# Which partitions an expert's 64 slots stand on: rank order against an order in which eight neighbours in rank lie four partitions apart

## The reference, cut to what matters

```python
gp = softmax(ht @ w_group + b_group);  p_top, g_idx = top_k(gp, 1)         # one group a token
el_sel = (ht @ w_expert + b_expert) of that group
top_l, e_idx = top_k(el_sel, 2)                                            # two experts in it
gates = one_hot(group) x (softmax(top_l) * p_top at e_idx)                 # 512 x 32
for each expert e:  z = silu(ht @ wg) * (ht @ wu);  y += gates[:, e] * (z @ wd)
```

## Time and profile before

| | |
|---|---|
| median of 3 runs | 1217.79 us |
| profiled execution | 1218.0 us, span 1216.3 us |
| TensorE matmul busy | 1144.7 us (94%) |
| VectorE / ScalarE / GpSimd busy | 528.5 / 425.1 / 205.8 us |
| memory read / written | 265.84 MB / 30.41 MB |
| mixture of layer 0 | from about 500 to 746 us of the span |
| mixture of layer 1 | from about 964 to 1208 us of the span |

### The profile page before, as it was taken

The page is one execution under the profiler, slowest core; times in us unless marked ns, Lnnn a source line. Parts: engine busy times, 40 slices in busy tenths (PEclk is TensorE's granted clock), DMA queues, the critical chain, the costliest instruction groups (busy, mean ns, idle before and its releaser), DMA issues.

```text
span 1216.3 us, 29422 instructions
## 1 busy us (share of the span) xinstructions
PE 1144.7 (94%) x12512; PEld 626.1 (51%) x12512; DVE 528.5 (43%) x988; ACT 425.1 (35%) x823; POOL 205.8 (17%) x234
## 2 busy tenths in 40 slices
PE   6999999999999989899998889999999999998885
PEld 5365555555555644555554445544554555554442
DVE  6756564664565510511111125899941511111125
ACT  5335354454453421322121124555443321211123
POOL 3000000000000000222221110688800112221110
PEclk9999999999999989999999999999999999999898
DMA  4017311011012168799999998226702889999996
GB/s 162 3 55 294 126 50 42 21 59 42 20 59 72 74 216 330 283 358 420 423 420 422 424 376 339 70 74 255 311 0 75 324 307 425 420 422 422 422 402 255
DMA packets 53779, 281.97 MB, mean 232 GB/s; under 512 B 14956, under 2 KB 17132, under 8 KB 36496
## 3 DMA queue, kind: packets, MB, share of 16 engines
q1 hardware_dynamic: 43952, 263.73, 54.2%
q0 software_dynamic: 9408, 16.32, 3.7%
q10 hardware_dynamic: 288, 0.03, 0.0%
HBM read 265.84 MB, written 30.41 MB: 244 GB/s over the span
## 4 chain that ended last, share of the span: by engine, by line
PE 79%; DMA 13%; DVE 3%; ACT 2%; issue 2%; SPq 1%; DVEq 0%
PE psum L1611 15%; PE psum L976 14%; PE psum L2145 9%; PE psum L2443 8%; PE psum L1792 6%; PE psum L989 6%; DMA h<-rows 5%; DMA big<-in_moe_w_gate_up_dram 4%; DMA h<-in_moe_w_gate_up_dram 4%; PE psum L943 2%; PE psum L1916 1%; PE psum L1781 1%; PE psum L2453 1%; SPq L424 1%; PE psum L2419 1%
## 5 line engine op out<-in xcount | busy, mean ns | idle before, releaser
L976 PE MATMUL psum<-big 128*64 128x256 f32 x1536 | 190.0, 391 | 22.4 <-issue 12.7
L1611 PE MATMUL psum<-big 128*128 128x512 f32 x384 | 191.2, 618 | 1.4 <-PE psum L1916 0.3
L976 PEld LDWEIGHTS psum<-big 128*64 128x64 f32 x1536 | 107.5, 139 | 91.3 <-issue 33.8
L1110 DVE SCALAR_TENSOR_TENSOR big<-psum,big 128x128 f32<-128x128 f32 x64 | 22.5, 351 | 292.7 <-ACT big L1060 292.7
L989 PE MATMUL psum<-big 128*64 128x512 f32 x512 | 120.9, 593 | 1.2 <-DMA big<-in_moe_w_down_dram 0.8
L2145 PE MATMUL psum<-big 128*128 128x512 f32 x256 | 116.5, 608 | 0.8 <-ACT big L2546 0.8
L896 POOL DMA_INDIRECT chosen<-big x60 | 59.9, 998 | 312.3 <-ACT big L1071 142.8
L1985 ACT COPY big<-psum 128x512 f32<-128x512 f32 (+1 forms) x112 | 69.1, 649 | 107.6 <-PE psum L1792 105.2
L2388 POOL TENSOR_TENSOR big<-big 128x512 f32<-128x512 f32 x76 | 96.7, 1272 | 36.0 <-ACT big L2528 25.5
L2443 PE MATMUL psum<-big,conv_w 128*128 128x512 f32 x224 | 96.5, 592 | 0.0
L1792 PEld LDWEIGHTS psum<-big 64*64 64x64 f32 x4096 | 71.6, 134 | 48.2 <-issue 47.2
(11 more groups left out here) (290 smaller groups left out, 1392.2 us busy)
## 6 DMA issues: line engine op xcount, KB each, us to landing
big<-in_moe_w_gate_up_dram SPq DMA_DIRECT2D x40, 2048.0 KB, 31.1
big<-in_moe_w_down_dram SPq DMA_DIRECT2D x64, 1024.0 KB, 27.7
conv_w<-in_moe_w_gate_up_dram SPq DMA_DIRECT2D x8, 2048.0 KB, 31.7
h<-in_moe_w_gate_up_dram SPq DMA_DIRECT2D x8, 2048.0 KB, 26.8
big<-in_moe_w_gate_up_dram SPq DMA_DIRECT2D x16, 1024.0 KB, 12.5
big<-in_rwkv_w_rkv_dram SPq DMA_DIRECT2D x24, 512.0 KB, 4.2
chosen<-h SPq DMA_DIRECT2D x8, 1024.0 KB, 12.6
conv_w<-in_conv_w_pw_dram SPq DMA_DIRECT2D x8, 1024.0 KB, 4.7
```

Source lines behind the costliest of these rows:

```text
L976: last = nc.tensor.matmul(o[half * SLOTS:(half + 1) * SLOTS, 0:F_EXP].rearrange("p (u f) -> p u f", u=2), m.xT[e // 2 % 2][:, c, (e % 2) * ...
L1611: last = nc.tensor.matmul(bank[b], m.w[:, n, c, :], x[:, c, :], start=(c == 0), stop=(c == C - 1))
```

## The change

The table `slot_of_col` is written by four instructions instead of one. In each half of 64 columns, column 4a + b of the lower 32 holds a + 8b (a from 0 to 7, b from 0 to 3), and column 32 + 4a + b holds 32 + a + 8b. So ranks 0 to 7 stand on partitions 0, 4, 8, ..., 28, ranks 8 to 15 on 1, 5, ..., 29, and so on; ranks 32 to 63 on partitions 32 to 63 in the same manner. The two halves of the table still hold the same. Nothing else changes: each table, the gate factors and the one-hot matrices are made from `hot` as before, with the same number and shapes of instructions.

```diff
-            st.done(nc.gpsimd.iota(slot_of_col[:], pattern=[[0, 2], [1, SLOTS]], base=0, channel_multiplier=0,
-                                   allow_small_or_imprecise_dtypes=True))
+            for half in range(2):
+                for upper in range(2):
+                    at = half * SLOTS + upper * SLOTS // 2
+                    st.done(nc.gpsimd.iota(slot_of_col[:, at:at + SLOTS // 2], pattern=[[1, 8], [8, 4]],
+                                           base=SLOTS // 2 * upper, channel_multiplier=0,
+                                           allow_small_or_imprecise_dtypes=True))
```

## The result

The changed kernel takes 1211.18 us (median of 5 runs, 1208.77 to 1213.71), against 1217.8 before: a ratio of 0.9948, 95% interval 0.9932 to 0.9964, or 6.6 us faster. 8.5 us were forecast.

The account below looks back on a forecast made before the run. The prediction took the most loaded DMA engine to bound the end of each mixture. Savings of 8.2 us there and 0.3 in the first gather, 8.5 from the profiled 1218.0, gave 1209.5, stated as 1209.3 us; range 1204 to 1215.

Parts of the forecast that it names:

- What bounds: End of each mixture: DMA engines set it, and 11.6 us of the span hang on the most loaded engine.
- The map: Indirect transfers: an engine owns four neighbouring partitions and the four 32 further on; excess 203 to 70 and 223 to 57 KB.
- What it saves: Mixture ends: 66% and 74% of the 5.1 and 6.5 us excess go, 3.4 and 4.8 us, together 8.2.
- The signs that the prediction named: Before `h<-rows` lands: share near 1 until some 5 us ahead, excess near 1.7 us per layer, start 3.4 and 8 sooner.
- rival D: Most loaded engine saves 133 and 166 KB at the full 0.044 us a KB: 13.2 us, 1204.6 us; chance 14%.
- On the path: TensorE's gaps from 640 us on shrink by the gain, none comes elsewhere, and the 0.94 us wait stays.
- First gather: Layer 0's first gather, 4.52 us on the chain: fullest engine has 6 rows instead of 8, 0.3 us saved.
- Setup: Three more table instructions on GpSimd at the start: about 0.3 us later, covered, so 0 in the sum.
- Landing times of gathers and scatters: Indirect transfers land sooner by about a fifth, at some 9 and 6.5 us, from 10.7 and 8.0.
- A (common ceiling): 422 GB/s is a ceiling shared by all engines, so balancing them is worth nothing: 1217.8 us; chance 9%.
- B (partition modulo 16): Partitions go to engines singly, so eight ranks fall on four engines and excess grows: 1223.3 us; chance 5%.
- C (runs of eight): Engines own eight neighbouring partitions, so the excess falls by only 25 and 47 KB, 3.2 us: 1214.6 us; chance 4%.

Follow-up runs that it names:

- the opposite order: Against the changed kernel, ranks 0 to 7 on partitions 0 to 3 and 32 to 35, the next eight on the following runs: 1241.80 us, 1.0182 of before.
- the four pieces alone: Against the kernel before, the table is written by four instructions but with the old values in rank order: 1218.18 us, 0.9995.
- the alternating order: Against the changed kernel, each next eight ranks go in turn to lower partitions and those 32 higher: 1210.41 us, 0.9944 of before.
- The reversed order: Against the changed kernel, the eight runs of partitions are taken from last to first, with equal counts: 1213.54 us, 0.9953 of before.

## Why the prediction was right, and by how much it was off

**What bounds.** Right. The end of each mixture hangs on the most loaded DMA engine; what was taken from its excess (2.6 and 3.8 us in the windows) came off the stretches (2.5 and 3.5 us), and the same holds for every order that was run but the opposite one: stretch minus excess stays within 213.3 to 214.1 us.

**The map.** Right. The flat stretch at 0.9 was thin evidence, and the opposite order turned it into a plain one: half of the engines free, 22 us slower, and the other half through in the order of their KB. That is the formula of the Trainium skill, page "DMA: Bandwidth & Descriptors", section "The descriptor swizzle"; the runs agree with it for indirect transfers too, as far as which partitions share an engine. Which engine has which number they don't show.

**What it saves.** The mechanism right, the size off: 3.4 and 4.8 us were forecast, 2.5 and 3.5 came in one profile and 2.4 and 2.0 in the other. The signs that the prediction named were off with it: the excess that is left was to be 1.7 us in each layer and is 2.3 to 3.9, the share was to hold until 5 us ahead of the landing and falls 6 to 7 us ahead, and `h<-rows` of layer 1 was to start 8 us sooner and starts 6.4 sooner. The step that was mis-sized is "the counts remove 66% and 74% of the excess", applied to the whole 5.1 and 6.5 us. The kernel that moves no rows shows about 2 us in each that the counts can't touch. Taken off, 0.66 x (5.1 - 2.1) = 2.0 and 0.74 x (6.5 - 1.9) = 3.4 us: 5.4, between the 6.0 and the 4.4 of the two profiles. Whether the two parts simply add, profiles that lie this far apart don't show. The other term of the sum, the full price of 0.044 us a KB and 13.2 us (rival D), was far off at this end, though 0.038 held at the other, where the counts dwarf the engines' own difference: from 299 KB come 6.0 us of the stretches, 0.020 a KB. By the full price, 203 and 223 KB would have been 8.9 and 9.8 us of excess before, and 4.9 and 6.6 were there. Where the rest went, the prediction guessed (rows moved before the engines are full) and no run tests.

**On the path.** Right in what it says of the bound: no gap came elsewhere, and the 0.94 us in front of the residual stayed, as this row of the changed kernel's TensorE shows:

```profile
728.85 1.55 PE L1009 MATMUL psum<-h,ident 128*128 128x512 f32 x3 [0.94 <-DMA h<-rows]
```

Only in half right that the gaps shrink by the gain: they shrank by 0.8 and 1.7 us, and the rest is busy time, part of it at the low clock.

**First gather.** 0.58 us in the first profile and 0.42 in the second (4.52 to 4.10), against 0.3; both inside the bound of 1.1 that a quarter of 4.52 gives.

**Setup.** 0.37 us later on GpSimd, forecast 0.3, covered as forecast: the four pieces alone are 0.9995.

**Landing times of gathers and scatters.** Wrong: a fifth less was expected (9 and 6.5 us), and 10.6 and 8.0 came. I took the landing time to follow the rows of the fullest engine. The run without rows shows that it hardly depends on rows at all (9.8 and 7.7 us). That it follows the turns of its packets among those of the weights, which the change leaves alone, would fit and isn't shown. It had no part in the sum.

**Rivals.** A (common ceiling) fell with the half-idle engines at 406 GB/s per full share. B (partition modulo 16) fell with the result, 1223.3 expected and 1211.2 measured, again with the opposite order (1211 expected, 1241.8 measured) and again with the alternating one. C (runs of eight) expected 1214.6, 3.4 above the result. In the opposite order its lower sixteen partitions and the sixteen 32 further on fill four of eight engines, as the old order did, so it expects the time of before, and the kernel is 22 us above it; in the alternating order it expects a large gain, and none came.

What stays open is where the engines' own 2 us come from, and how they combine with the rows. The reversed order didn't tie them to the end of the eight, and the 16 steps don't say which engine is which.

## What to carry to other kernels

When loads stream at full rate, look at the DMA share in single microseconds ahead of a landing that something waits for: a share that falls early says that the engines are not evenly loaded, and 1 minus the share, summed, is the most that evening them out can give, as long as nothing else becomes the bound. Where gathers and scatters leave rows out, put the filled rows so that neighbours in rank fall on different engines (here: four partitions apart), and count rows per engine, not per transfer. Before such a sum is trusted, measure what is uneven without those rows and subtract it; here it was a third of the excess.

## What the runs showed of the hardware

- Eight filled slots in a row on one engine's partitions, instead of spread over eight, cost 30 us between two kernels that issue the same instructions (1241.8 against 1211.2).
- Leaving rows of an indirect transfer out of bounds takes away their bytes and no packet: 9408 packets with 16.32 MB and with 0.07 MB. Two neighbouring half rows of 2 KB share a packet in a scatter: the packets under 512 B fall by 188 and 298 in two orders, as the counts give for pairs.
- As long as the DMA engines set the end of a mixture, its length is a constant plus the lag of the last engine behind the mean: 213.3 to 214.1 us plus 1.5 to 6.6, in 16 mixtures.
- The landing time of an indirect transfer beside a full stream of weights hardly depends on its rows: 9.8 to 11.1 us for gathers from no rows to all rows on half of the engines, 7.7 to 8.3 for scatters. The last of these is the row of the kernel with eight ranks in one run:

```profile
chosen<-big POOLq DMA_INDIRECT x60, 8.3
...
big<-rows,big POOLq DMA_INDIRECT x32, 11.1
```

- Sixteen engines with equal bytes are not through together: with next to no rows the last is 2.2 and 1.7 us behind the mean at the end of a mixture (about 100 MB of loads), and 3.9 and 3.3 us behind the first.
